# Two attention mixers of a transformer kernel: half chunks padded to 128 rows, low parts on GpSimd, another order of stick-breaking and index rounds

## The reference

```python
def hybrid_mixer(h, w_in, b_forget, g_kv, w_kv_up, g_idx_k, w_up_fox, w_up_sb, w_up_dsa, w_out, cos, sin):
    (q_a, k_a, v_a, f_a, q_b, k_b, v_b, q_c, c_kv, q_i, k_i, w_i, gates) = jnp.split(h @ w_in, ...)
    y_a = forgetting_attention(q_a, k_a, v_a, f_a + b_forget)         # "fox", 6 heads of 64
    y_b = stick_breaking_attention(q_b, k_b, v_b)                     # 5 heads
    ...
    y_c = dsa_attention(q_c, k_c, v_c, q_i, k_i, w_i)                 # 5 heads, keys chosen by an index
    g_a, g_b, g_c = jnp.split(jax.nn.sigmoid(gates), N_BRANCH, axis=-1)
    merged = g_a * (y_a @ w_up_fox) + g_b * (y_b @ w_up_sb) + g_c * (y_c @ w_up_dsa)
    return merged @ w_out
```

## Time and profile before

| | |
|---|---|
| median of 3 runs | 2757.98 us (2754.88 to 2762.97) |
| profiled execution | 2758.39 us, its span 2756.4 us, mean granted clock 0.958 |
| TensorE matmuls | busy 2602.2 us (94%) |
| VectorE | 1367.5 us (50%) |
| ScalarE | 1144.9 us (42%) |
| GpSimd | 303.6 us (11%) |
| mixer of layer 0, from chunk 3's end to the start of w_out | 1698.4 to 1872.0 us |
| the same in layer 1 | to 2529.5 us; its merges from 2483.4 |

### The profile page before, as it was taken

How to read it: one execution, slowest core, us unless ns; L and a number is a source line. 1 busy time by engine, 2 the same in 40 slices (tenths; PEclk the granted TensorE clock), 3 DMA queues, 4 the chain that set the end, 5 groups by cost and what they waited for, 6 DMA issues and landing times.

```text
span 2756.4 us, 41454 instructions
## 1 busy us (share of the span) xinstructions
PE 2602.2 (94%) x17370; PEld 2281.8 (83%) x17370; DVE 1367.5 (50%) x2351; ACT 1144.9 (42%) x1970; POOL 303.6 (11%) x292
## 2 busy tenths in 40 slices
PE   4997999899999899989999998999999999999998
PEld 2763677677777687779999997889999998887998
DVE  2234434333333424555566556646556656665654
ACT  3242444322122424554454444445445444444543
POOL 1132411200000002410010000111000000022000
PEclk6997999899999889989999999989999999999999
DMA  5412222244443222235465452325545554333544
GB/s 223 177 54 94 75 77 92 92 183 164 180 183 132 90 85 90 80 123 183 167 207 184 168 193 99 131 100 170 184 168 198 179 173 155 115 118 137 182 166 140
DMA packets 60184, 393.44 MB, mean 143 GB/s; under 512 B 6688, under 2 KB 6848, under 8 KB 23520
## 3 DMA queue, kind: packets, MB, share of 16 engines
q1 hardware_dynamic: 59328, 384.45, 39.8%
q0 software_dynamic: 672, 6.36, 0.6%
HBM read 389.73 MB, written 1.05 MB: 142 GB/s over the span
## 4 chain that ended last, share of the span: by engine, by line
PE 83%; ACT 7%; DVE 6%; issue 2%; POOL 2%; DMA 1%; SPq 0%; DVEq 0%; POOLq 0%; ACTq 0%
PE ps L822 69%; PE ps L900 4%; DVE ring_lo L1459 3%; PE ps L972 2%; PE ps L863 2%; PE ps L957 2%; PE ps L946 1%; ACT w_hi L1109 1%; ACT logits L1249 1%; ACT prob_t L1164 1%; PE ps L873 1%; DMA ring<-w_mod 1%; PE ps L922 1%; DMA ring<-w_w_in 1%; PE ps L913 0%
## 5 line engine op out<-in xcount | busy, mean ns | idle before, releaser
L1459 DVE TENSOR_TENSOR ring_lo<-ring,w_hi 128x1024 fp32r<-128x1024 f32 (+3 forms) x712 | 764.6, 1115 | 553.1 <-ACT w_hi L1109 552.9
L822 PE MATMUL ps<-h_hi,w_hi 128*128 128x256 f32 (+1 forms) x3408 | 963.3, 314 | 30.5 <-ACT h_hi L1154 26.3
L822 PE MATMUL ps<-h_lo,w_hi 128*128 128x256 f32 (+1 forms) x3408 | 934.8, 307 | 0.0
L1109 ACT ACTIVATE w_hi<-ring 128x1024 fp32r<-128x1024 f32 (+3 forms) x712 | 642.7, 950 | 580.4 <-PE ps L822 232.8
L822 PEld LDWEIGHTS ps<-h_hi,w_hi 128*128 128x128 f32 x3408 | 654.5, 193 | 90.1 <-issue 31.0
L822 PEld LDWEIGHTS ps<-h_lo,w_hi 128*128 128x128 f32 x3408 | 652.7, 193 | 27.9
L822 PE MATMUL ps<-h_hi,ring_lo 128*128 128x256 f32 (+1 forms) x3408 | 558.3, 307 | 0.0
L822 PEld LDWEIGHTS ps<-h_hi,ring_lo 128*128 128x128 f32 x3408 | 484.8, 192 | 28.6
L822 PE MATMUL ps<-hid_hi,w_hi 128*128 128x256 f32 (+1 forms) x1056 | 284.2, 302 | 0.0
L822 PE MATMUL ps<-hid_lo,w_hi 128*128 128x256 f32 (+1 forms) x1056 | 283.4, 301 | 0.0
L1393 POOL TENSOR_SCALAR logits<-logits,stat 128x512 f32<-128x512 f32 (+2 forms) x140 | 161.3, 1165 | 738.2 <-DVE stat L1689 738.2
(11 more groups left out here) (222 smaller groups left out, 2435.8 us busy)
## 6 DMA issues: line engine op xcount, KB each, us to landing
ring<-w_ffn_in SPq DMA_DIRECT2D x132, 1024.0 KB, 4.8
ring<-w_ffn_out SPq DMA_DIRECT2D x96, 704.0 KB, 4.0
ring<-w_mod SPq DMA_DIRECT2D x48, 1024.0 KB, 6.8
ring<-w_in SPq DMA_DIRECT2D x42, 1024.0 KB, 4.8
ring<-w_w_in SPq DMA_DIRECT2D x30, 1024.0 KB, 4.9
ring<-w_up SPq DMA_DIRECT2D x16, 576.0 KB, 3.6
ring<-w_pab SPq DMA_DIRECT2D x8, 1024.0 KB, 4.8
ring<-w_wo SPq DMA_DIRECT2D x8, 1024.0 KB, 4.7
```

The lines of the kernel that those rows point to most:

```text
L822: mm = pe.matmul(ps[f.bank][:, 0:n], (hi_w if wpart == "hi" else lo_w)[0:rows, at:at + P], hi if part == "hi" else lo, start=left == first ...
L1109: act.activation(w_hi[q.s % 2][:, h * n:(h + 1) * n], ring[q.slot][:, h * n:(h + 1) * n], ACT.Copy)\
L1459: dve.tensor_tensor(ring_lo[q.slot][:, c], ring[q.slot][:, c], plain(w_hi[q.s % 2][:, c]), ALU.subtract)\
```

## The change

It has four parts, in both layers of the second block.

1. Rows 64 to 127 of y's chunks 5 and 8 are set to zero once a layer (`dve_y2_pad`, two memsets after chunk 14), the y_split of these chunks handles 128 rows (and waits for the memsets), and all matmuls of the merges have 128 rows.
2. `tok vb` computes and copies 330 columns in place of 384.
3. `merged_rest` is GpSimd's: for m ≥ 1 the low part of m−1 comes after the second add of m, and at m = 7 that of 7 follows too.
4. The items between tile 3 and the last gate tile stand in another order. A third and a fourth index round stand behind tile 3 and behind tile 5; stick_ln is between tiles 4 and 5; four rounds and index_end stand together behind `tok va`; stick_acc, stick_pv and fox are spread from there to gate tile 3; attention starts at gate tile 4, so that 14 of its 16 calls stand in the gates and two behind them.

Tiles are numbered by chunk: the piece `chunks(i)` makes tiles 2i and 2i+1, with `next(t)` the first of them and with `run_all(t)` the rest.

```diff
-            add("stick_ln", n=5 * l, zs=zs)
+            add("index_round")
             t = chunks(2)
             next(t)
-            stick_acc(0, 1)
+            add("stick_ln", n=5 * l, zs=zs)
+            run_all(t)
+            add("index_round")
             fox(0)
-            run_all(t)
-            stick_acc(2, 3, 4)
-            fox(1)
+            stick_acc(1)
             tok(f"va{l}", w["va2"][l], 2, 4 * 384, 384, S, va2, scaled=True)
-            sv = [fill(V_BANK) for _ in range(3)]
-            for i, fv in enumerate(sv):
-                add("stick_pv", i=i, f=fv, n=5 * l)
-            fox(2, 3)
+            for _ in range(4):
+                add("index_round")
+            add("index_end", n=count("sel"))
+            stick_acc(0, 3)
...
             for u in range(12):
                 for c in feat(f"2g{l}", f[9 + u], [2 * u, 2 * u + 1], S):
                     if c == 0:
+                        stick_acc(2)
+                        fox(1)
+                    elif c == 1:
+                        stick_acc(4)
+                        stick_pv(0)
+                        fox(2)
+                    elif c == 2:
+                        stick_pv(1)
+                        fox(3)
+                    elif c == 3:
+                        stick_pv(2)
                         fox(4, 5)
-                    if 1 <= c <= 6:
-                        add("index_round")
-                    if c == 7:
-                        add("index_end", n=count("sel"))
-                    if c and c % 3:
+                    elif c % 3:
+                        if c < 6:
+                            stick_split(c - 4)
                         att(g)
+                    elif c == 6:
+                        stick_split(2)
             att(g, 16)
@@ pe_merge2
-                        rows = DH if c in (5, 8) else P
-                        terms.append((c * P, y2_hi[0:rows, c * S:(c + 1) * S], y2_lo[0:rows, c * S:(c + 1) * S], rows, c))
+                        terms.append((c * P, y2_hi[:, c * S:(c + 1) * S], y2_lo[:, c * S:(c + 1) * S], P, c))
@@ pool_merge2
                 pool.tensor_tensor(tmp[0][:, o], tmp[0][:, o], tmp[2][:, o], ALU.add).then_inc(mg_full, 1)
+                if m:
+                    merged_rest(st["mg"] - 1, m - 1)
+                if m == KC - 1:
+                    merged_rest(st["mg"], m)
+
+            def merged_rest(n, m):
+                pool.wait_ge(mg_hi_ready, n)
+                o = slice(m % 2 * S, (m % 2 + 1) * S)
+                pool.tensor_tensor(at_T(mg2_lo, m, S), tmp[0][:, o], plain(at_T(mg2_hi, m, S)), ALU.subtract).then_inc(mg_ready, 1)
@@ dve_merge2
-                if m:
-                    merged_rest(st["mg"] - 1, m - 1)
-                if m == KC - 1:
-                    merged_rest(st["mg"], m)
@@ pe_tok
-                                mm = pe.matmul(ps[f.bank][:, 0:cols], at_T(part, c, T, t * P, P), wt[:, at:at + cols],
+                                mm = pe.matmul(ps[f.bank][:, 0:st["n"]], at_T(part, c, T, t * P, P), wt[:, at:at + st["n"]],
@@ second_block
+            add("y2_pad", after=fc(14))
-            tok(f"vb{l}", w["vb2"][l], 2, 4 * 384, 384, S, vb2, scaled=True)
+            tok(f"vb{l}", w["vb2"][l], 2, 4 * 384, 384, S, vb2, scaled=True, n_out=330)
@@ act_y_split
                 taken(st["after"])
+                if st["pad"]:
+                    act.wait_ge(pad_ready, st["pad"])
@@
+            def dve_y2_pad(st):
+                full(st["after"])
+                for c in (5, 8):
+                    ins = dve.memset(y2[DH:P, c * S:(c + 1) * S], 0.0)
+                ins.then_inc(pad_ready, 1)
```

More of the change, by code:

```diff
@@ L362, in tok @@
             feats[name, 0] = fs[-1]
-            add("tok", pieces=ps_, cols=cols, T=T, dst=dst, fs=fs, scaled=scaled)
+            add("tok", pieces=ps_, cols=cols, T=T, dst=dst, fs=fs, scaled=scaled, n=n_out or cols)
         def gate_up(src, i, T, fresh=None, norm=None, scaled=False):
@@ L401, in att @@
                     return
-                for c, rows, args in g["split"]:
-                    add("y_split", args=args, rows=rows, n=count("y"), after=c["V"])
+                for c, args in g["split"]:
+                    add("y_split", args=args, n=count("y"), after=c["V"], pad=c.get("pad"))
                 g["split"] = []
@@ L411, in att @@
                     if p["done"]:
-                        g["split"].append((p, DH * p["heads"], p["done"]))
+                        g["split"].append((p, p["done"]))
                 if 2 <= i < len(steps) + 2:
@@ L697, in second_block, with stick_pv, stick_split @@
             run_all(t)
-            add("stick_ln", n=5 * l, zs=zs)
+            add("index_round")
             t = chunks(2)
             next(t)
-            stick_acc(0, 1)
+            add("stick_ln", n=5 * l, zs=zs)
+            run_all(t)
+            add("index_round")
             fox(0)
-            run_all(t)
-            stick_acc(2, 3, 4)
-            fox(1)
+            stick_acc(1)
             tok(f"va{l}", w["va2"][l], 2, 4 * 384, 384, S, va2, scaled=True)
-            sv = [fill(V_BANK) for _ in range(3)]
-            for i, fv in enumerate(sv):
-                add("stick_pv", i=i, f=fv, n=5 * l)
-            fox(2, 3)
+            for _ in range(4):
+                add("index_round")
+            add("index_end", n=count("sel"))
+            stick_acc(0, 3)
+            sv = [None] * 3
+            def stick_pv(i):
+                sv[i] = fill(V_BANK)
+                add("stick_pv", i=i, f=sv[i], n=5 * l)
+            def stick_split(i):
+                add("y_split", args=y2_of(3 + i), n=count("y"), after=sv[i], pad=l + 1 if i == 2 else None)
             def y2_of(c):
-                return tuple(a[0:DH if c in (5, 8) else P, c * S:(c + 1) * S] for a in (y2, y2_hi, y2_lo))
+                return tuple(a[:, c * S:(c + 1) * S] for a in (y2, y2_hi, y2_lo))
             def fox_pair(i):
@@ L722, in dsa_pair @@
                             v=lambda c, h: vc2[:, c * DH:(c + 1) * DH], rope=plan.counts["rope"], sel=l + 1, done=y2_of(6 + i),
-                            y=y2[:, (6 + i) * S:(7 + i) * S], causal=True, bias=lambda h, t: t * S, wide=False)
+                            y=y2[:, (6 + i) * S:(7 + i) * S], causal=True, bias=lambda h, t: t * S, wide=False,
+                            pad=l + 1 if i == 2 else None)
             g = attention([fox_pair(i) for i in range(3)] + [dsa_pair(i) for i in range(3)])
-            for i in range(3):
-                add("y_split", args=y2_of(3 + i), rows=DH if i == 2 else P, n=count("y"), after=sv[i])
-            done = -1
             for u in range(12):
@@ L1185, in act_tok @@
                     full(f)
-                    act.activation(st["dst"][:, t * st["cols"]:(t + 1) * st["cols"]], ps[f.bank][:, 0:st["cols"]], ACT.Copy,
+                    act.activation(st["dst"][:, t * st["cols"]:t * st["cols"] + st["n"]], ps[f.bank][:, 0:st["n"]], ACT.Copy,
                                    scale=rstd[:, t:t + 1] if st["scaled"] else 1.0).then_inc(psum_taken[f.bank], 1)
@@ L1744, in dve_merge2 @@
                     dve.tensor_tensor(tmp[b][:, o], ps[f.bank][:, 0:S], gates2(8 * b + m), ALU.mult).then_inc(psum_taken[f.bank], 1)
-                if m:
-                    merged_rest(st["mg"] - 1, m - 1)
-                if m == KC - 1:
-                    merged_rest(st["mg"], m)
-            def merged_rest(n, m):
-                dve.wait_ge(mg_hi_ready, n)
-                o = slice(m % 2 * S, (m % 2 + 1) * S)
-                dve.tensor_tensor(at_T(mg2_lo, m, S), tmp[0][:, o], plain(at_T(mg2_hi, m, S)), ALU.subtract).then_inc(mg_ready, 1)
             def dve_fox_ls(st):
@@ L1837, in _ @@
                       head_spread=dve_head_spread, rope=dve_rope, att=dve_att, y_split=dve_y_split, merge1=dve_merge1,
-                      merge2=dve_merge2, fox_ls=dve_fox_ls, fox_bias=dve_fox_bias, index=dve_index, index_caps=dve_index_caps,
+                      merge2=dve_merge2, y2_pad=dve_y2_pad, fox_ls=dve_fox_ls, fox_bias=dve_fox_bias, index=dve_index, index_caps=dve_index_caps,
                       index_round=dve_index_round, index_end=dve_index_end, stick_z=dve_stick_z, stick_ln=dve_stick_ln,
```

4 lines of the change are left out of this document (2 added, 2 removed).

## The result

The changed kernel takes 2743.12 us (median of 5 runs, 2741.60 to 2748.98) where the one before takes 2757.98 us: a ratio of 0.9949, 95% interval 0.9934 to 0.9965, 0.5% faster. 2745 us was forecast. Its profiled execution has a span of 2743.8 us, 12.6 less than before.

The account below looks back on a forecast made before the run. TensorE was taken as nearly the bound in the q/k and gate stages, a 5.83 us cycle outside it in the merges. Layer 0 −9.7, layer 1 −4.65, together −14.35, +1.6 for half clock: −12.7 from 2758.4, 2745 us; range 2734 to 2758.

Parts of the forecast that it names:

- The cycle of 5.83 us: Merge loop: a cycle through ScalarE, VectorE and GpSimd sets each turn at 5.83 us, so padding's saving there is waiting.
- 24.4 us: Merges: ceiling of padding's saving by TensorE's spacing, 1.53 us for one m, over sixteen; TensorE-bound rival's chance 0.07.
- Cover at half clock: Merges: padded matmuls at half clock need 5.75 us a turn, which fits under 5.83.
- The 4.5 us of the earlier trace: Layer 0's merges: 4.5 us lost in three slow turns under half clock, which padding need not lose.
- slower by the clock: Rival: idling TensorE brings half clock into w_out and FFN, 9 us per stretch; above 2766 us, chance 0.06.
- 330 columns: Tile of v_b: 48 matmuls of 330 columns, not 384, save 1.1 us a layer, counted −2.2.
- The new order: q/k and gate stages: waits fall from 12.7 to 6.4 us; gates end 7.5 (layer 0) and 7.9 us (layer 1) earlier.
- my +1.6: New order: one of its four waits of 2.3 to 2.4 us is followed by a half-clock stretch, costing +1.6 us.
- The tail: Attention's end now behind the gates: mg_hi(0) at +9.7, w_out at +49.7 us; layer 1 +3.65, layer 0 −0.9.
- Low parts on GpSimd: Merged rows: no gain in the loop; at w_out's start layer 1 +0.7 us, layer 0 −0.2 us.

Follow-up runs that it names:

- pipe: Changed kernel with ScalarE making mg_hi of m-1 after the sigmoids and weight conversion of m: 2721.20 us, ratio to the kernel before 0.9862.
- pipe_no_pad: pipe with the padding undone (64 rows in chunks 5 and 8, no memsets): 2727.22 us, ratio to the kernel before 0.9885.
- no_pad: Changed kernel with the padding undone (64 rows in chunks 5 and 8, no memsets): mixers of 282.2 and 290.1 us.
- reorder_only: Kernel before with only the new order, the fourth part of the change: mixers of 284.4 and 291.0 us, −7.1 and −0.4.
- att16: Changed kernel with all 16 attention steps inside the gate tiles: mixers of 279.3 and 287.2 us, −3.0 and +0.3.
- best_att16: pipe2_lo_dve with all 16 attention steps inside the gate tiles: 2704.73 us, ratio to the kernel before 0.9808.
- lo_dve: Changed kernel with the low parts of the merged rows back on VectorE: mixers of 282.0 and 287.1 us, −0.4 and +0.2.
- pipe2: pipe with the sigmoids of m+1 also put in front of mg_hi of m-1: 2722.48 us.
- pipe2_lo_dve: pipe2 with the low parts of the merged rows on VectorE: 2709.08 us once, then 2712.59 us over 5 runs, ratio to the kernel before 0.9839.

## Why the prediction was right, and where not

**The cycle of 5.83 us.** It rested on the earlier trace rows and on the equal turns of layer 1. It holds in every kernel that keeps the order of mg_hi, with 64 or 128 rows, low parts here or there, and is gone in pipe. This was the decision that mattered: by TensorE's spacing the padding promised 24.4 us. That price was right: the unpadded turn of pipe_no_pad takes 4.76 us, where 4.8 was worked out (the six affected gaps of a branch are seven, 0.21 to 0.31 us each; their sum is the 0.763). The changed kernel got none of it at full clock: layer 0's merges take 47.8 us with padding and in no_pad. Only padding alone, on the kernel before, gained 1.05 us a layer in the first turn, which my expectation for it lacked.

**Cover at half clock.** The 4.5 us of the earlier trace rows went in the changed kernel, and 3.2 came back in no_pad and 3.3 in reorder_only, in layer 1 that time. In ten profiles of padded kernels (twenty merges) the mean clock in the merges was 0.89 or more; in the eight merges of profiled unpadded kernels it was 0.78 to 0.80 in three. So what I called cover was never put to the test: no padded turn lay under such a stretch, and that it would still take 5.83 us there rests on 27 × 0.213 alone. Whether padding, which makes TensorE idle more there, keeps the long slow stretch away isn't shown by this, only that it never stood there; that the 4.5 us went may be chance. My rival "slower by the clock" is not seen.

**330 columns.** −1.0 us on the chain, 1.1 forecast (0.153 us between starts, 0.151 worked out).

**The new order.** Forecast −7.5 and −7.9 without v_b; measured −6.6 and −7.3 by the table. Waits over TensorE's own pace in layer 1 of the changed kernel: 1.5 before stick_acc(1) (1.2 forecast), 2.4 in v_a (2.4), 2.4 before stick_acc(2) (2.3), 0.45 at tile 2 (0.5). In layer 0 the third was 1.2, because a stretch at half clock lay over v_a before it:

```profile
1711.10:1714.50 3.40, 3.38 (x11) 3.40 (x12) 1.53 (x2) 2.00 (x2) 0.00 (x0) 0.53 0.52 145
```

That TensorE then arrives later and waits less is what my +1.6 for such a stretch left out, since VectorE's four rounds set the end either way. From the end of the wait in v_a to the matmul ahead of the next wait layer 0 took 10.26 us, where layer 1 took 8.78: the stretch cost 1.5. The next wait was 1.2 us shorter, so about 0.25 were left. The term that was mis-sized is this +1.6; the 0.9 and 0.6 us that the order gave less than forecast cancel it, and that is luck.

**The tail.** Forecast mg_hi(0) at +9.7 and w_out at +49.7 after the gates, +3.65 in layer 1 and −0.9 in layer 0; measured 9.56, 49.6, +3.4 and −1.1. att16 shows it from the other side, and best_att16 what it is worth once the loop is opened (7.9 us in both layers). It is the largest loss inside the change.

**Low parts on GpSimd.** Forecast: nothing in the loop, +0.7 and −0.2 at the end. Measured by lo_dve: nothing in the loop, 0 to 0.2 at the end. The page "SBUF — State Buffer" of the Trainium skill (section "SBUF: two separate sides") has a VectorE operation with two SBUF inputs and a GpSimd operation that reads SBUF lock each other out of a shared port pair. In the changed kernel no meeting stands on the path; in pipe they meet each turn, and the rows of 1.97 and 1.25 us beside 1.43 and 0.74 agree with it. The single records do, too: VectorE's first instruction ends at 2475.06, GpSimd's add, begun at 2474.41, at 2475.66, and VectorE's second, begun at 2474.98, at 2476.27, each some 0.6 us behind the one before. Which part of the 0.61 us a turn between pipe2 and pipe2_lo_dve is the port and which the wait on the two halves of `tmp` stays open; the chain names the wait.

**The total.** 2745 forecast, 2743.12 measured; the mixers gained 13.6 us against 14.35 forecast before the +1.6, and 12.7 with it. With it the gate stages came out at −15.8 for −16.0, by the luck named above; the 0.9 us more are the tail (+2.3 for +2.75) and w_out's first tile (−0.1 for +0.5). That the profiled execution took 2745.62 us, for 2745.7 forecast, is luck again: it began 1.0 us late.

## What to carry to other kernels

When an engine is busy 90% of a loop, look for equal spacing of one operation of another engine before crediting it with time saved: a turn that keeps to the hundredth of a microsecond is set by a cycle of waits, and only an edit that cuts this cycle moves it. Walk the cycle to its next holder before cutting (mg_hi, then the buffer's two halves, then VectorE's own sum): each was hidden behind the one before, and where two branches of a cycle end within 0.15 us of each other, the one that the profile names need not be the one that holds it. An edit that costs nothing under one can cost 4 us a layer under the next. Work moved behind the last cover (here two attention steps behind the gate tiles) starts the next stage's whole chain later, so count it by the chain it holds up, not by its own 1.2 us.
